# Both PSUM halves of a routed expert's output copied by ScalarE, none by VectorE

## What is computed

```
def body(acc, blk):
    toks, bw, e = blk
    xb = hp[toks]
    yb = (jax.nn.silu(xb @ w_gate[e]) * (xb @ w_up[e])) @ w_down[e]
    return acc.at[toks].add(yb.astype(f32) * bw[:, None]), None
```

## Time and profile before

| What | us |
|---|---|
| median of three runs | 2513.45 |
| lowest, highest | 2511.47, 2514.35 |
| the profiled execution, its own time | 2510.86 |
| span of the profiled execution | 2509.0 |
| granted TensorE clock, mean | 0.973 |

### The profile page before, as it was taken

How to read it: one execution, slowest core, us unless ns; L and a number is a source line. 1 busy time by engine, 2 the same in 40 slices (tenths; PEclk the granted TensorE clock), 3 DMA queues, 4 the chain that set the end, 5 groups by cost and what they waited for, 6 DMA issues and landing times. The chain is left out here.

```text
span 2509.0 us, 49346 instructions
## 1 busy us (share of the span) xinstructions
PE 2357.9 (94%) x11266; PEld 1904.2 (76%) x11268; DVE 1758.6 (70%) x2382; ACT 1179.1 (47%) x1863; POOL 972.2 (39%) x772
## 2 busy tenths in 40 slices
PE   8899999999998799999999999999999999999966
PEld 6576777678886677888778887787778888877855
DVE  6686767758878767667767677667766677767437
ACT  3525253532225545455554545545554546545334
POOL 0010100011110155554555555554655556555437
PEclk9999999979998899999999999999999999999988
DMA  6143434465655478878887878888888789887796
GB/s 252 76 168 122 137 116 141 136 222 196 216 206 208 167 240 269 248 220 271 254 269 232 260 232 247 272 261 257 255 241 249 226 240 300 274 247 229 180 248 202
DMA packets 165327, 551.13 MB, mean 220 GB/s; under 512 B 31344, under 2 KB 56080, under 8 KB 144784
## 3 DMA queue, kind: packets, MB, share of 16 engines
q1 hardware_dynamic: 109696, 355.03, 40.1%
q0 software_dynamic: 54960, 195.27, 31.0%
q10 hardware_dynamic: 608, 0.02, 0.0%
HBM read 394.99 MB, written 155.25 MB: 219 GB/s over the span
## 5 line engine op out<-in xcount | busy, mean ns | idle before, releaser
L2647 PE MATMUL psG<-gu_split,xT_hi 128*128 x2624 | 626.0, 391 | 3.4 <-ACT xT_hi L2421 1.9
L2647 PEld LDWEIGHTS psG<-gu_split,xT_hi 128*128 128x128 f32 x2624 | 494.9, 189 | 107.5 <-issue 4.1
L1669 POOL DMA_INDIRECT xg<-hcut,gi x332 | 376.6, 1134 | 144.0 <-issue 92.5
L2661 PE MATMUL psG<-gu_split,xT_lo 128*128 x1304 | 341.2, 403 | 0.0
L2526 DVE TENSOR_TENSOR gu_split<-raw_gu,gu_split (+1 forms) x127 | 289.4, 2279 | 69.2 <-ACT gu_split L2444 59.5
L2406 POOL DMA_INDIRECT acc<-y,si x81 | 170.4, 2104 | 413.1 <-DVE y L2602 376.5
L2661 PEld LDWEIGHTS psG<-gu_split,xT_lo 128*128 128x128 f32 x1304 | 233.1, 189 | 42.4
L2444 ACT ACTIVATE gu_split<-raw_gu x126 | 234.4, 1908 | 33.2 <-issue 16.6
L2510 DVE STREAM_TRANSPOSE xF<-xg 128x1024 f32<-128x1024 f32 x82 | 177.2, 2161 | 91.8 <-DMA xg<-hcut,gi 91.7
L2526 DVE TENSOR_TENSOR d_lo<-raw_d,d_hi (+1 forms) x64 | 146.6, 2291 | 123.9 <-ACT d_hi L2444 123.9
L2699 PE MATMUL psY<-d_hi,HT_lo 128*128 x648 | 204.3, 397 | 18.8 <-DVE HT_lo L2589 18.8
(11 more groups left out here) (404 smaller groups left out, 4038.9 us busy)
## 6 DMA issues: line engine op xcount, KB each, us to landing
raw_gu<-in_w_gate_dram SPq DMA_DIRECT2D x64, 1024.0 KB, 5.2
raw_gu<-in_w_up_dram SPq DMA_DIRECT2D x64, 1024.0 KB
raw_d<-in_w_down_dram SPq DMA_DIRECT2D x64, 1024.0 KB
wring<-split_d SPq DMA_DIRECT2D x24, 1024.0 KB, 5.8
second<-blank SPq DMA_DIRECT2D x17, 512.0 KB, 6.8
split_d<-wring POOLq DMA_DIRECT2D x8, 1024.0 KB, 4.2
raw_d<-mixed SPq DMA_DIRECT2D x16, 512.0 KB, 5.3
xt<-in_x_dram SPq DMA_DIRECT2D x16, 512.0 KB, 5.7
```

What stands on the lines that cost most here:

```text
L1669: nc.gpsimd.indirect_dma_start(out=to[:, g, 0:PIECE], out_offset=None, in_=hcut.rearrange("r a w -> (r a) w"), in_offset=bass.IndirectOffs ...
L2647: nc.tensor.matmul(psG[slot][:], xT_hi[slot][:, c, :], right[:, bass.ds(w, 1), c, :].rearrange("p a n -> p (a n)"), start=(n == 0 and c == ...
L2661: m = nc.tensor.matmul(psG[slot][:], xT_lo[slot][:, c, :], gu_hi[:, bass.ds(w, 1), c, :].rearrange("p a n -> p (a n)"), start=False, stop= ...
```

## The change

ScalarE copies the second half of y too, behind its own half and ahead of the branch with `d_hi`. The copy waits for `yps_s[1]`. VectorE's copy is gone with its two waits; the wait for the scatter of the turn before (`added[k]`) stands on ScalarE already, in `scatter_index`. Both semaphores of the copies count as before, so TensorE and GpSimd wait for the same numbers.

```diff
--- before.py
+++ after.py
@@ -2494,6 +2494,8 @@
                     s.wait(act, yps_s[0])
                     scatter_index(s, k)
                     nc.scalar.activation(y[k][:, 0:512], psY[:, 0, :], ACT.Copy).then_inc(y_s[0], 1)
+                    s.wait(act, yps_s[1])
+                    nc.scalar.activation(y[k][:, 512:], psY[:, 1, :], ACT.Copy).then_inc(y_s[1], 1)
                     when_first(act, nexts[n], lambda: split_down(nexts[n], s.n + 1))
 
             turns(act, body)
@@ -2597,9 +2599,6 @@
                     if k == 0:
                         turn_x(s.turn + 2)
                     when_first(dve, nexts[n + 1], lambda: split(nexts[n + 1], 0))
-                    s.wait(dve, yps_s[1])
-                    dve.wait_ge(added[k], s.turn * 16)
-                    nc.vector.tensor_copy(y[k][:, 512:], psY[:, 1, :]).then_inc(y_s[1], 1)
                     when_first(dve, nexts[n + 1], lambda: split(nexts[n + 1], 1))
                     when_first(dve, nexts[n], lambda: split(nexts[n], 2))
```

## The result

The changed kernel takes 2544.35 us, the median of four runs (2543.42 to 2544.81), beside 2513.9 for the kernel before, now the median of four: a ratio of 1.012, 95% interval 1.0104 to 1.0136. Forecast were 2485 us and 0.89 for faster. The kernel is 30 us slower, and the mechanism was none of the rivals as they were priced.

A forecast was written before the change was run, and what follows sets the result against it. TensorE bounds the kernel; its 59.9 us idle ahead of the down product's first and third pairs is the ceiling. 28.1 + 4.2 - 3.9 = 28.4 us won, from a median of 2513.45 to 2485 us, range 2468 to 2504.

The forecast's parts named there:

- the sum: Expert phase: 28.1 us (late turns) + 4.2 (`HT_lo` waits) - 3.9 (later `d_hi`) = 28.4 us won.
- the 21 late ones: Two-step turns where a late gather reaches TensorE, 1.96 us each: 13.1 us lost in place of 41.2, 28.1 won.
- the 15 with `HT_lo` late alone: Turns with `HT_lo` late by 0.32 us but no late gather: 0.28 x 15 = 4.2 us, all won.
- the 26 with the down split in the even step: Later `d_hi` delays the next step's `HT_lo`, so TensorE's third pair waits: 0.15 x 26 = 3.9 us lost.
- the loop: y copy, scatter, next gathers, next `xF`, next y copy: earlier copy cuts a late turn's 1.96 us loss to 0.47 or 0.93.
- the 59.9: Ceiling of the win: TensorE's idle ahead of the down product's first pair, 26.8 us, and third pair, 33.1 us.
- (a): Weight loads of gate and up set the gathers' landing: turns of 19.20 us, 13 us won, 2500.5; chance 0.2.
- (b): Scatter takes 1.59 us at its new place, so no late turn is left: 41.5 us won, 2472; chance 0.14.
- The delay of `d_hi`: On ScalarE, the branch now comes behind the waiting copy: `d_hi` 0.45 us later, bounds 0.11 and 1.03.
- The step that failed: Pricing `d_hi`'s delay by the third pair's wait for `HT_lo` alone: 0.15 us in 26 even-step down splits.
- these two: Down product's first weight pair, waiting for y copies (26.8 us), and third pair, waiting for `HT_lo` (33.1 us).
- Rival (c): Split chain becomes the bound: `d_hi` later by 1.46 us cancels the gain, 1.9 gives 2534 us; chance 0.05.

The follow-up runs named there:

- e14: The change, plus twelve more SyncE table loads ahead of each load of down weights (4 to 8 us later): 2472.65 us, 0.9871, chip D.
- e18: The kernel before, with the down weights' load some 7 us later: 2508.52 us, 0.9996, chip E.
- e6: The kernel before, with two small ScalarE copies of constants ahead of `d_hi` in even steps, making it late: 2545.55 us, 1.0156, chip C.
- e7: The change, plus a 512-column memset on GpSimd ahead of the gathers of odd steps: 2484.04 us, 0.9895, chip C.
- e16: The change, plus a memset on GpSimd ahead of the scatter of odd steps: 2492.15 us, 0.9931, chip E.
- e5: The change, but ScalarE makes `d_hi` ahead of its copy of the second half: 2485.82 us, 0.9912, chip B.
- e8: The change, but with `d_hi` ahead of ScalarE's second copy in even steps alone: 2487.5 us, 0.9922, chip C.
- e17: The change, with the down weights' load some 7 us later: 2538.07 us, 1.0113, chip E.
- e1: The change, but VectorE keeps its old waits at their old place, with a one-column memset for the copy: 2522.32 us, 1.0067, chip B.
- e9: The kernel before, with one more SyncE table load ahead of each load of down weights: 2507.81 us, 1.0000, chip C.
- A: The first comparison, recorded without its chip: the change against the kernel before, 2544.35 beside 2513.9 us, 1.012.
- e2: The change in even steps only; in odd steps VectorE copies the second half as before: 2515.95 us, 1.0035, chip B.
- e12: The change, with GpSimd's gathers of odd steps waiting for VectorE's `HT_lo` of the same step: 2478.92 us, 0.9890, chip D.
- e19: The change, with GpSimd's gathers of odd steps waiting for `HT_lo`, run again on chip F: 2479.74 us, 0.9903.

## Why the prediction was wrong

**The gain: the sum held, partly by luck.** e14 is the change with a load moved, on a chip without the stall; the load was worth nothing in the kernel before (e18). It is 30.7 us faster than the kernel before on that chip (2503.36 against 2472.65); the sum said 28.4. Beside the trace of the kernel before, from another group, its phase takes 1461.5 us against 1490.6, 29.1 less. The terms can be told apart by adding up turns in these two traces, and they are off in both directions:

| turns | forecast won | before | e14 | won |
|---|---|---|---|---|
| the 21 late ones | 28.1 | 420.0 | 396.1 | 23.9 |
| the 15 with `HT_lo` late alone | 4.2 | 271.4 | 268.4 | 3.0 |
| the 26 with the down split in the even step | -3.9 | 469.7 | 467.3 | 2.4 |

What fell short is the loop: the late turn of the earlier trace rows takes 18.74 us in the change and not 18.3, and the next `xF` starts 3.0 us into its step (1593.60 against 1590.64) and not 2.5. Ahead of the first and the third pair e14 idles 1.2 and 23.8 us, 34.9 less than the 59.9 of the earlier trace rows:

```profile
L2701 PEld LDWEIGHTS psY<-d_hi,HT_lo 128*128 128x128 f32 x648 | 119.0, 188 | 49.0 <-issue 23.8
L2701 PEld LDWEIGHTS psY<-d_hi,HT_hi 128*128 128x128 f32 x648 | 120.6, 188 | 28.1 <-issue 1.2
```

Rivals (a) and (b) did not come.

**The delay of `d_hi` was sized right, and what the third pair pays for it nearly.** `d_hi` starts 0.79 us after the copy's start (0.9 said) and was to be 0.45 late: it is 0.4. `HT_lo` starts at 0.46 (0.5 said) in the 26 steps, and the third pair at 0.99 in place of 0.91 in e14, 0.08 later where 0.15 was said.

**The step that failed** is the price of those 26 steps: "0.15 x 26 = 3.9 us lost". It asked only how long TensorE's third pair waits for `HT_lo`. It did not ask what else on VectorE's queue moves behind `d_lo`, and what that meets on GpSimd: the gathers were taken to be served alike wherever they begin. With it falls the close of the first paragraph, "All that follows is about what makes these two late": a place where TensorE never waited (`gate_up_low`) was costed at nothing without naming its cover. Estimated from two traces, the change's and e14's, the stall costs 1531.5 - 1461.5 = 70 us. Of these 202.2 - 142.3 = 59.9 lie in the fifteen steps and 135.3 - 126.2 = 9.1 in the even steps just behind them. Rival (c) had the right suspect, a later `d_hi`, but the wrong price and the wrong path: it needed 1.46 us by its sum, through TensorE's wait for `HT_lo`, and 0.4 was enough through GpSimd's queue.

**What is shown, and what is open.** Shown: the stall follows from a later `d_hi` without any copy moved (e6); it goes, with `d_lo` as late, when pieces and scatter are issued later (e7, and within it step by step; e16 in part), and when `d_hi` is early again (e5, e8); it does not need the down weights' load beside it (e17) or VectorE's run ahead (e1). Chip or group matters as well, and each chip was seen in one group only: on B, C and E TensorE's signals come late in some odd steps in every kernel traced, on D and F in none of six kernels. In the kernel before with a moved load they come late as well (e18, e9) and cost next to nothing. The two traces of A do not settle it: the kernel before has no late signal in any step, the change has them in 54. That TensorE's sequencer is caught in the change because it is itself 0.39 us later there (its first instruction of the step comes at 0.92 and not 0.53, as it waits for `HT_lo` ahead of the third pair) fits, but was tried only on a chip without late signals. What holds the sequencer, and what differs between the chips, stays open.

**A better version.** `d_hi` ahead of the copy (e5, 0.9912) and the memset ahead of the gathers (e7, 0.9895) are faster than the kernel before on chips where signals are late and where a kernel with the late `d_hi` stalled beside them (e1 and e2; e6). Gathers behind `HT_lo` (e12, e19: 0.9890 and 0.9903) are faster than the kernel before on two chips where signals aren't late, but e14, the change but for the load, is as fast there (0.9871), so they have not shown more.

## What to carry to other kernels

When an edit delays one operation by a few tenths, follow the whole queue behind it, and also the other engine's operation that will now overlap it or no longer will: here 0.4 us on ScalarE became 0.7 us *earlier* on GpSimd. Where an engine has no wait in the trace, ask how much lead its sequencer has before costing a shift at nothing. And give each group of runs the changed kernel as its control, beside the kernel before: four kernels seemed to be cures; beside the control one of them was none, one held in part, and two were never tried where the stall is.

## What the runs showed of the hardware

**One kernel, two chips, both signs.** The change with the far load: 0.9871 on D, 1.0113 on E. The medians of the kernel before stay within 2503 to 2514 us in all six comparisons. Each chip was used in one group, so that the chip makes the difference, and not the hour, is likely but not shown.

**VectorE beside GpSimd's gather.** Here it matters which of the two starts first. The first piece took 1.69 us where `xT_lo` had started 0.39 us ahead of it (1454.59) and 0.99 where both started together (1463.76), though `xT_lo` then ran beside the whole of it. The 1.69 us end 0.86 us behind the end of `xT_lo`, and the 1.95 us of e7, where `xT_lo` had started 0.14 ahead, end 0.87 behind it, as if most of the issue's work began when `xT_lo` was done. With the scatter's 2.68 and 1.59 us that is a second pair of rows in which the issue is longer where a VectorE operation from SBUF to SBUF is already running. The Trainium skill, SBUF — State Buffer, Who interferes with whom, infers that descriptor generation is not hit; these rows disagree.

**A stall mostly costs twice.** Busy time by stretch after, with the granted clock in the last column but two:

```profile
1463.00:1474.00 11.00, 7.97 (x41) 6.53 (x39) 4.34 (x9) 3.12 (x8) 5.45 (x5) 1.00 1.05 296
1474.00:1481.00 7.00, 6.27 (x15) 4.95 (x16) 2.03 (x2) 1.92 (x2) 0.98 (x1) 0.51 0.37 99
```

And the eight products of `gate_up_low` in the late turn:

```profile
1578.63 2.10 PE L2660 MATMUL psG<-gu_split,xT_lo 128*128 x8
```

After the 3.94 us without work the granted clock is 0.51, the lower of the two levels (1.2 GHz), and the eight products of `gate_up_low` take 3.78 us; at the full clock, in the late turn, they take 2.10. It is not so behind every stall: of the fourteen over 2 us in the trace after, the eight weight loads of `gate_up_low` take 2.2 us or more behind eleven and 1.7, as at the full clock, behind three (stalls of 2.3 to 2.8 us), and behind the 3.11 us of e7 the granted clock stays at 1.00. In the kernel before the granted clock is 1.00 in each third of the phase from 900 us on, in the change 0.98, 0.99 and 0.98.
